# The chunked recurrence of a transformer block: its inverse's turned form made by transposes in each level

## The chip, the cores and the metric

One core of one Trainium2 chip runs the whole program in one launch. The metric is device time in microseconds, the median of three runs of the kernel. TensorE is called PE below, and its weight loads PEld; VectorE is DVE in the profile's rows, ScalarE ACT, GpSimd POOL.

## What is computed

The program is two transformer blocks over 512 tokens (with 256 context tokens in front in the second). One part of the second block's mixer is a linear recurrence with a removal term, run over 768 tokens in both directions for 8 heads of 64 dims:

```python
def wkv7_scan(state0, r, w, k, v, a_vec, b_vec, reverse):
    def step(S, inp):
        r_t, w_t, k_t, v_t, a_t, b_t = inp
        sa = jnp.einsum('bhij,bhj->bhi', S, a_t)
        S = (S * w_t[:, :, None, :] + sa[..., None] * b_t[:, :, None, :]
             + v_t[..., None] * k_t[:, :, None, :])
        return S, jnp.einsum('bhij,bhj->bhi', S, r_t)
```

The rest (norms, projections, three kinds of attention, experts) stands unchanged in both kernels.

## The kernel before, in words

Stage `Wkv` does this recurrence in 12 steps of 64 tokens. Within a step the 64 tokens depend on one another through a strictly triangular 64x64 matrix per head and direction, of which (1 - L) has to be inverted. There are 16 such matrices (4 pairs of heads `c`, 2 heads `e` of a pair, 2 directions `d`), kept in tiles of 128 partitions by 512 columns, and a group of 16 products of 64x64 works on all of them; in the trace a group is 32 matmul records. The inverse X is built in 5 levels: the blocks of L that join neighbours of size 2, 4, 8, 16, 32 (`lo`, made by GpSimd, "level_blocks") are multiplied by X (`half`, L2211), ScalarE copies the result out of PSUM (`t1`, L2373), a second product multiplies it by X from the other side (`grow`, L2224), and VectorE adds it to X (L2468). As a matmul takes its left operand transposed, `grow` needs X turned. So the kernel before keeps X twice: plain in `x` and turned in `xt`. `grow_turned` (L2232) makes the addition to `xt`, and VectorE adds it (L2471). The last level makes only the turned form.

Around the levels stand, in the order in which PE runs a step: three turns of value, replacement and key factors to token rows (`turn`, L2184, copied by ScalarE, L2369); `key_grams` (L2169, masked by VectorE, L2460); in level 0 `gram(2)` (L2161, mask L2420); in levels 1 to 4 products beside the half products that need only the state or the values (`w_from_state` L2250, `w_from_keys` L2274, `y_from_state` L2258); then the first two grams of the next step (L2161, masks L2420 and L2427), the solved values u (L2307), a turned gram of the next step (L2178, mask L2433), and the products into outputs and state (L2266, L2317, L2321, L2325). VectorE adds state (L2439) and outputs (L2452) and decays the state (L2445). VectorE also makes the factors of the next step: `removal` L2407, `reading` L2412, `replacement` L2416, `new_keys` L2402.

The order on each engine is the order of the code; semaphores with counts by step and place tie the engines (`at`, `wait`), and PE runs the steps as a loop, with waits against registers. In the kernel before, the tiles of `lo`, `x`, `xt` and `t1` have their two directions placed so (`home`) that the four products in a row use the four quarters of PE. PE's products onto the diagonal quarters alone (rows to the same columns, as in `grow_turned`) use two.

The level, on PE and on VectorE:

```python
for lv in range(self.LEVELS):
    half(lv)
    ...
    ready(lv)
    if lv < last_lv:
        grow(lv)
    grow_turned(lv)
```

## Time and profile before

| | us |
|---|---|
| median of 3 runs | 2858.52 (2855.38 to 2859.93) |
| the profiled execution | 2863.22 |
| its span, first to last instruction | 2861.4 |
| PE matmuls busy, share of the span | 2508.4, 88% |
| PE weight loads | 1945.2, 68% |
| VectorE | 1637.7, 57% |
| ScalarE | 1215.2, 42% |
| GpSimd | 426.4, 15% |
| mean granted clock of TensorE | 0.930 |

The profile is of one execution. Busy shares are averages over many stages; the stage `Wkv` stands at 1362 to 1644 us of the span, about a tenth of it, and only its own rows tell what bounds it. In a timeline row the first number is the start in us from the span's start, the second the time from the first instruction's start to the last one's end, then engine, line, operation, output and inputs, shape and count; in brackets the engine's idle time before and what ended it ("issue": nothing that the profile shows). PE's records overlap, so a group's time is longer than the distance to the next group's start.

### The profile page before, as it was taken

What the parts mean: (1) busy time and instruction counts of PE and PEld (TensorE: products, weight loads), DVE (VectorE), ACT (ScalarE), POOL (GpSimd) and SP (SyncE); (2) the same over time, 40 slices, a digit from 0 to 9 for tenths busy, and PEclk for the clock granted to TensorE, in tenths of its full rate; (3) what the DMA queues carried; (4) which work ended last, traced back from release to release, by engine and by line L of the source; (5) the groups of instructions that cost most, each with busy time, mean ns of one, the idle gap of its engine ahead of it and who ended that gap; (6) DMA issues with size and microseconds to landing.
All of it is one profiled execution on the core that took longest, in us unless ns stands there. A gap on an engine that the chain in (4) does not pass through costs nothing.

```text
span 2861.4 us, 55427 instructions
## 1 busy us (share of the span) xinstructions
PE 2508.4 (88%) x23264; PEld 1945.2 (68%) x23264; DVE 1637.7 (57%) x2360; ACT 1215.2 (42%) x1740; POOL 426.4 (15%) x412
## 2 busy tenths in 40 slices
PE   6979889999978779997888887899977889988996
PEld 5745577787857436785888765777766656767774
DVE  3655535555442274445566564588965355548895
ACT  2433333222231216424333324278864247446784
POOL 1010001000010020002455401122220030012221
PEclk9978989999999779998999988999988899999997
DMA  4246922222211000100000031199863100017995
GB/s 176 89 154 254 351 87 96 96 88 97 93 61 45 25 0 1 78 16 5 2 0 0 10 139 61 68 385 378 339 263 133 66 1 2 25 70 286 355 345 199
DMA packets 63892, 353.33 MB, mean 123 GB/s; under 512 B 15329, under 2 KB 15345, under 8 KB 27248
## 3 DMA queue, kind: packets, MB, share of 16 engines
q1 hardware_dynamic: 41792, 292.60, 26.9%
q0 software_dynamic: 21936, 58.50, 5.5%
q8 instruction: 109, 1.79, 0.2%
q14 instruction: 55, 0.45, 0.0%
HBM read 344.91 MB, written 36.70 MB: 133 GB/s over the span
## 4 chain that ended last, share of the span: by engine, by line
PE 72%; DVE 8%; ACT 5%; issue 4%; PEld 3%; DVEq 3%; DMA 2%; POOL 1%; POOLq 1%; ACTq 1%; PEldq 1%
PE psum L642 13%; PE psum L436 12%; PE psum L3271 9%; PE psum L3293 4%; PE psum L1187 4%; PE psum L1827 3%; PE psum L1206 3%; PE psum L1197 3%; PE psum L2882 2%; PEld psum L436 2%; PE psum L2232 2%; PE psum L1733 2%; PE psum L2211 1%; PE psum L3236 1%; PE psum L1045 1%
## 5 line engine op out<-in xcount | busy, mean ns | idle before, releaser
L436 PE MATMUL psum<-arena_r 128*128 128x512 f32 (+1 forms) x976 | 312.3, 361 | 4.3 <-DVE weight_slots_r L462 4.2
L642 PE MATMUL psum<-arena_r 128*128 128x512 f32 x704 | 250.8, 397 | 10.8 <-issue 4.0
L436 PE MATMUL psum<-arena_r,weight_slots_r 128*128 128x512 f32 (+1 forms) x696 | 249.1, 358 | 0.0
L457 ACT ACTIVATE arena_r<-weight_slots 128x1024 fp32r<-128x1024 f32 x73 | 76.4, 1057 | 334.5 <-PE psum L436 251.1
L642 PE MATMUL psum<-arena_r,weight_slots_r 128*128 128x512 f32 x528 | 209.1, 396 | 0.0
L436 PEld LDWEIGHTS psum<-arena_r 128*128 128x128 f32 x976 | 179.3, 190 | 36.0 <-issue 4.3
L436 PE MATMUL psum<-h_t_r,arena_r 128*128 128x512 f32 (+1 forms) x528 | 192.7, 365 | 0.0
L3225 DVE TENSOR_TENSOR weight_slots_r<-weight_slots,arena_r 128x2048 fp32r<-128x2048 f32 x78 | 177.6, 2290 | 20.1 <-ACT arena_r L3220 19.7
L3225 DVE TENSOR_TENSOR weight_slots_r<-weight_slots,h_t_r 128x2048 fp32r<-128x2048 f32 x72 | 163.9, 2290 | 20.9 <-ACT h_t_r L3220 20.8
L642 PEld LDWEIGHTS psum<-arena_r 128*128 128x128 f32 x704 | 133.8, 190 | 45.6 <-issue 13.6
L1271 DVE TENSOR_REDUCE stat<-psum 128x1 f32<-128x768 f32 (+1 forms) x112 | 98.7, 881 | 108.1 <-PE psum L1187 107.9
L3271 PE MATMUL psum<-weight_slots_r,arena_r 128*128 128x512 f32 x400 | 157.7, 394 | 0.0
L3220 ACT ACTIVATE arena_r<-weight_slots 128x2048 fp32r<-128x2048 f32 x78 | 148.2, 1919 | 17.4 <-DMA weight_slots<-in_weights 16.7
L436 PEld LDWEIGHTS psum<-arena_r,weight_slots_r 128*128 128x128 f32 x696 | 131.7, 189 | 20.3
L3220 ACT ACTIVATE h_t_r<-weight_slots 128x2048 fp32r<-128x2048 f32 x72 | 136.8, 1920 | 17.4 <-DMA weight_slots<-in_weights 16.9
L3271 PE MATMUL psum<-arena_r 128*128 128x512 f32 x416 | 132.2, 399 | 10.1 <-issue 7.5
L642 PE MATMUL psum<-h_t_r,arena_r 128*128 128x512 f32 x352 | 140.3, 399 | 0.0
L1187 PE MATMUL psum<-arena 64*128 64x384 f32 (+2 forms) x416 | 121.0, 532 | 8.6 <-POOL arena L1237 4.9
L3271 PE MATMUL psum<-h_t_r,arena_r 128*128 128x512 f32 x384 | 122.5, 400 | 5.7 <-issue 5.7
L642 PEld LDWEIGHTS psum<-arena_r,weight_slots_r 128*128 128x128 f32 x528 | 100.2, 190 | 22.6
L462 DVE TENSOR_TENSOR weight_slots_r<-weight_slots,arena_r 128x1024 fp32r<-128x1024 f32 x73 | 88.4, 1219 | 45.2 <-ACT arena_r L457 44.3
L3379 POOL DMA_INDIRECT arena<-h_rows,arena x50 | 71.7, 1435 | 274.1 <-PE psum L3236 190.0
(469 smaller groups left out, 5485.0 us busy)
## 6 DMA issues: line engine op xcount, KB each, us to landing
weight_slots<-in_weights SPq DMA_DIRECT2D x277, 1024.0 KB, 6.8
arena<-y_rows POOLq DMA_DIRECT2D x20, 512.0 KB, 7.9
h_rows<-arena POOLq DMA_DIRECT2D x10, 512.0 KB, 2.9
x_keep<-x_t POOLq DMA_DIRECT2D x1, 3072.0 KB, 9.0
x_t<-x_keep POOLq DMA_DIRECT2D x2, 1536.0 KB, 8.6
x_t<-in_x POOLq DMA_DIRECT2D x1, 2048.0 KB, 9.8
out_x<-x_t SPq DMA_DIRECT2D x1, 2048.0 KB, 7.2
arena<-in_toe POOLq DMA_DIRECT2D x1, 1792.0 KB, 7.3
```

The costliest lines, as they stand in the source:

```text
L436: last = self.nc.tensor.matmul(self.bank(n), w[:, kt, :], self.operand(part, kt, a, b), start=(i == 0), stop=(i == len(passes) - 1))
L462: self.nc.vector.tensor_tensor(out=self.tile_weights(self.kern.slots_r, t), in0=self.tile_weights(self.kern.slots, t), in1=self.w_hi[:, t ...
L642: last = nc.tensor.matmul(bank, w(p, k), x(q, k), start=(k == j == 0), stop=(k == n - 1 and j == 2))
L1187: last = t_.matmul(s[:, r, a:b], q, key[:, a:b], start=True, stop=True)
L1197: last = t_.transpose(self.turned_bank(u)[:, i * P:(i + 1) * P], self.probs[:, u % 2, i * P:(i + 1) * P], kern.ident)
L1206: last = t_.matmul(self.out_bank()[64 * e:64 * e + 64, :], self.units[u][2](i), self.probs_t[:, u % 4, i * P:(i + 1) * P], start=(i == 0), ...
L1271: v.reduce_max(kern.row_max[:, par], self.score_bank(u), mybir.AxisListType.XY)
L1827: last = self.nc.tensor.matmul(self.bank(n), w, x, start=(i == 0), stop=(i == len(pairs) - 1))
L3220: self.nc.scalar.activation(self.weights(item)[0], x, ACT.Copy).then_inc(self.rounded[0], 1)
L3225: self.nc.vector.tensor_tensor(out=self.kern.slots_r[:, slot, :], in0=self.kern.slots[:, slot, :], in1=hi.bitcast(F32), op=ALU.subtract).t ...
L3271: last = nc.tensor.matmul(ps[t % 2], x[:, t % 2, kt * P:(kt + 1) * P], w[:, k, :], start=(kt == 0 and i == 0), stop=(kt == KT - 1 and i == 2))
L3293: last = nc.tensor.matmul(ps[5 + half], x[:, t % 2, k * P:(k + 1) * P], w[:, k, half * 512:(half + 1) * 512], start=(k == 0 and i == 0), s ...
```

## The change

Only `Wkv` changes. X is kept plain alone. At the start of every level four 128x128 transposes on PE (`turned`) write X turned into PSUM bank 6, and VectorE copies that bank to `xt` when the half product is done (`turned_copied`); `grow` waits for this copy and for ScalarE's. `grow_turned`, its addition in each level, the turned gram of the next step and the second preset by GpSimd are gone; the last level multiplies onto the turned form and VectorE adds it to `xt`. The three turns, the key grams and the last gram move from the front of the step into the levels (`beside`): key grams at level 0, last gram and the turns of replacement factors and values at level 1, the keys' turn at level 3. The state product moves to level 2 and needs the decayed state; the value product stands whole at level 3. On VectorE the copies are new, removal stands in level 3, the new keys in level 2, the reading factor behind the first masks of the next step. GpSimd's `keyed` moves from level 2 to level 3. The placement by `home` is gone.

```diff
         def step(n, more):
             def half(lv):
-                if lv:
-                    wait("level_added", n, self.sum_of(lv - 1, 0))
-                else:
-                    wait("token_rows", n, 1)
-                wait("level_blocks", n, lv)
-                for c, e, d in units:
-                    last = t.matmul(bank_of(6, d, c, e, self.home(c, d)), self.plain(w.lo[lv % 2], c, e, d), self.plain(w.x, c, e, d),
-                                    start=True, stop=True)
+                for c in range(4):
+                    for e, d in corners:
+                        last = t.matmul(into(4, 0, d, c, e), self.by_token(w.lo[lv % 2], c, d, e), self.by_token(w.x, c, d, e),
+                                        start=True, stop=True)
                 last.then_inc(self.sem("level_half"), 1)
 
-            def ready(lv):
+            def turned():
+                for c in range(4):
+                    t.transpose(self.turned_bank()[:, c * P:(c + 1) * P], w.x[:, c * P:(c + 1) * P], ident)
+
+            def grow(lv):
                 wait("level_half_copied", n, lv)
-                if lv:
-                    wait("level_added", n, self.sum_of(lv - 1, 1))
-                else:
-                    wait("state", n, -2)
-
-            def grow(lv):
-                for c, e, d in units:
-                    last = t.matmul(bank_of(4, self.home(c, d), c, e, d), self.turned(w.xt, c, e, d), self.turned(w.t1, c, e, d),
-                                    start=True, stop=True)
+                wait("level_turned_copied", n, lv)
+                for c in range(4):
+                    for e, d in corners:
+                        if lv < last_lv:
+                            last = t.matmul(into(4, 0, e, c, d), self.by_dim(w.xt, c, d, e), self.by_dim(w.t1, c, d, e), start=True,
+                                            stop=True)
+                        else:
+                            last = t.matmul(self.by_dim(self.turned_bank(), c, d, e), self.by_dim(w.t1, c, d, e),
+                                            self.by_dim(w.xt, c, d, e), start=True, stop=True)
                 last.then_inc(self.sem("level_summed"), 1)
 
-            def grow_turned(lv):
...
-            wait("more_factors", n)
-            turn(6, w.vc)
-            turn(7, w.bt)
-            wait("y_added", n, -1)
-            turn(0, w.kt)
-            wait("masked", n, 2)
-            wait("read", n)
-            key_grams().then_inc(self.sem("more_grams"), 1)
-            for lv in range(self.LEVELS):
-                half(lv)
...
+            def beside(lv):
                 if lv == 0:
-                    wait("token_rows", n, 2)
-                    gram(2).then_inc(self.sem("last_grams"), 1)
+                    wait("more_factors", n)
+                    wait("read", n)
+                    wait("state", n, -2)
+                    key_grams().then_inc(self.sem("more_grams"), 1)
                 if lv == 1:
+                    wait("y_added", n, -1)
+                    last_gram().then_inc(self.sem("more_grams"), 1)
+                    wait("more_masked", n, 0)
+                    turn(3, w.bt)
+                    turn(2, w.vc)
+                if lv == 2:
                     w_from_state()
-                if lv == 2:
-                    w_from_keys(0)
                 if lv == 3:
-                    w_from_keys(1)
+                    w_from_keys()
+                    turn(2, w.kt)
                 if lv == last_lv:
                     y_from_state()
-                ready(lv)
-                if lv < last_lv:
-                    grow(lv)
-                grow_turned(lv)
+
+            for lv in range(self.LEVELS):
+                wait("level_blocks", n, lv)
+                if lv:
+                    wait("level_added", n, lv - 1)
+                turned()
+                half(lv)
+                beside(lv)
+                grow(lv)
             if more:
+                wait("token_rows", n, 2)
                 first_grams(n, 1)
...
+        def rows(n, i, bank, x):
+            act.wait_ge(*self.at("tokens", n, i))
+            s.activation(x, psum[:, bank, :], ACT.Copy).then_inc(self.sem("token_rows"), 1)
+
         def step(n):
-            for i, (bank, x) in enumerate(((6, w.vr), (7, w.br), (0, w.kr))):
-                act.wait_ge(*self.at("tokens", n, i))
-                s.activation(x, psum[:, bank, :], ACT.Copy).then_inc(self.sem("token_rows"), 1)
             more = n + 1 < self.STEPS
             for lv in range(self.LEVELS):
-                act.wait_ge(*self.at("level_half", n, lv))
-                s.activation(self.two(w.t1), self.by_rows(6), ACT.Copy).then_inc(self.sem("level_half_copied"), 1)
+                half_copied(n, lv)
                 if lv == 0 and more:
                     decays(n + 1)
-                if lv == 1 and more:
-                    growths(n + 1)
+                if lv == 1:
+                    if more:
+                        growths(n + 1)
+                    rows(n, 0, 3, w.br)
+                    rows(n, 1, 2, w.vr)
                 if lv == 2 and more:
                     scaled(n + 1, 0, 1, 2, 3)
                 if lv == 3:
-                    act.wait_ge(*self.at("w_summed", n, 2))
-                    s.activation(self.four(w.wv), self.by_head(0, 0), ACT.Copy).then_inc(self.sem("w_copied"), 1)
-            act.wait_ge(*self.at("u_summed", n))
-            s.activation(self.two(w.uv), self.by_rows(6), ACT.Copy).then_inc(self.sem("u_copied"), 1)
+                    act.wait_ge(*self.at("solve_summed", n, 1))
+                    s.activation(self.four(w.wv), self.pair(0, 0), ACT.Copy).then_inc(self.sem("solve_copied"), 1)
+                    rows(n, 2, 2, w.kr)
...
+        def turned_copied(n, lv):
+            dve.wait_ge(*self.at("level_half", n, lv))
+            v.tensor_copy(w.xt, self.turned_bank()).then_inc(self.sem("level_turned_copied"), 1)
+
+        def grown(n, lv):
+            dve.wait_ge(*self.at("level_summed", n, lv))
+            if lv < self.LEVELS - 1:
+                last = v.tensor_tensor(out=self.four(w.x), in0=self.four(w.x), in1=self.pair(4, 0), op=ALU.add)
+            else:
+                last = v.tensor_tensor(out=w.xt, in0=w.xt, in1=self.turned_bank(), op=ALU.add)
+            last.then_inc(self.sem("level_added"), 1)
...
         def step(n):
             more = n + 1 < self.STEPS
-            dve.wait_ge(*self.at("more_grams", n))
-            for i, (dst, m) in enumerate(((w.lkt, w.strict), (w.rkt, w.incl))):
-                v.tensor_tensor(out=self.four(dst), in0=self.key_grams(i), in1=spread(m), op=ALU.mult)
-            dve.drain().then_inc(self.sem("more_masked"), 1)
             for lv in range(self.LEVELS):
+                turned_copied(n, lv)
                 if lv == 0:
-                    dve.wait_ge(*self.at("last_grams", n))
-                    mask(2, w.rbt, w.incl).then_inc(self.sem("more_masked"), 1)
-                if lv < self.LEVELS - 1:
-                    dve.wait_ge(*self.at("level_summed", n, self.sum_of(lv, 0)))
-                    v.tensor_tensor(out=self.two(w.x), in0=self.two(w.x), in1=self.by_rows(4), op=ALU.add).then_inc(
-                        self.sem("level_added"), 1)
-                dve.wait_ge(*self.at("level_summed", n, self.sum_of(lv, 1)))
-                v.tensor_tensor(out=w.xt, in0=w.xt, in1=psum[:, 3, :], op=ALU.add).then_inc(self.sem("level_added"), 1)
-                if lv in (1, 2) and more:
-                    if lv == 1:
-                        dve.wait_ge(*self.at("exps", n + 1))
-                        dve.wait_ge(*self.at("w_summed", n, 0))
-                    removal(n + 1, lv - 1)
+                    key_masks(n)
+                if lv == 3 and more:
+                    removal(n + 1)
+                grown(n, lv)
+                if lv == 1:
+                    last_mask(n)
+                if lv == 2 and more:
+                    new_keys(n + 1)
                 if lv == 3 and more:
                     replacement(n + 1)
             if more:
-                dve.wait_ge(*self.at("w_summed", n, 3))
-                reading(n + 1, 0)
-                reading(n + 1, 1)
-                dve.drain().then_inc(self.sem("read"), 1)
                 low(n + 1)
-                new_keys(n + 1)
-                up(n + 1)
+                reading(n + 1)
             state(n)
             outputs(n)
             decayed(n)
...
         def keyed(n):
             if n:
-                pool.wait_ge(*self.at("last_grams", n - 1))
+                pool.wait_ge(*self.at("tokens", n - 1, 1))
...
-                if lv == 2 and n + 1 < self.STEPS:
+                if lv == 3 and n + 1 < self.STEPS:
                     keyed(n + 1)
```

PE at the front of a step and in level 0, before (L2201 are waits against registers; L2184 are the turns, L2169 the key grams, L2211 the half product):

```order
L2201 REGISTER_ALU [waits wkv_more_factors]
L2184 MATMUL psum<-consts,arena 128x128 x8
L2201 REGISTER_ALU [waits wkv_y_added]
L2184 MATMUL psum<-consts,arena 128x128 x4
L2201 REGISTER_ALU [waits wkv_masked]
L2201 REGISTER_ALU [waits wkv_read]
L2169 MATMUL psum<-rstd,arena 64x128 x16
L2201 REGISTER_ALU [waits wkv_token_rows]
L2201 REGISTER_ALU [waits wkv_level_blocks]
L2211 MATMUL psum<-arena 64x64 x16
```

And now (L2164 the waits; L2181 are the transposes, L2175 the half product, L2139 the key grams, L2189 the growth):

```order
L2164 REGISTER_ALU [waits wkv_level_blocks]
L2181 MATMUL psum<-consts,arena 128x128 x4
L2175 MATMUL psum<-arena 64x64 x16
L2164 REGISTER_ALU [waits wkv_more_factors]
L2164 REGISTER_ALU [waits wkv_read]
L2164 REGISTER_ALU [waits wkv_state]
L2139 MATMUL psum<-rstd,arena 64x128 x16
L2164 REGISTER_ALU [waits wkv_level_half_copied]
L2164 REGISTER_ALU [waits wkv_level_turned_copied]
L2189 MATMUL psum<-arena 64x64 x16
```

The half product stood behind three turns and the key grams; it now stands behind four transposes alone, and the key grams stand between it and the growth.

PE in level 1 before, from the wait for the addition (L2250 the state product, L2224 the growth, L2232 the turned growth):

```order
L2201 REGISTER_ALU [waits wkv_level_added]
L2201 REGISTER_ALU [waits wkv_level_blocks]
L2211 MATMUL psum<-arena 64x64 x16
L2201 REGISTER_ALU [waits wkv_more_masked]
L2250 MATMUL psum<-arena,rstd 64x64 x16
L2201 REGISTER_ALU [waits wkv_level_half_copied]
L2201 REGISTER_ALU [waits wkv_level_added]
L2224 MATMUL psum<-arena 64x64 x16
L2232 MATMUL psum<-arena 64x64 x16
```

And now (L2146 the last gram, L2152 the turns of replacement factors and values):

```order
L2164 REGISTER_ALU [waits wkv_level_blocks]
L2164 REGISTER_ALU [waits wkv_level_added]
L2181 MATMUL psum<-consts,arena 128x128 x4
L2175 MATMUL psum<-arena 64x64 x16
L2164 REGISTER_ALU [waits wkv_y_added]
L2146 MATMUL psum<-rstd,arena 64x64 x16
L2164 REGISTER_ALU [waits wkv_more_masked]
L2152 MATMUL psum<-consts,arena 128x128 x8
L2164 REGISTER_ALU [waits wkv_level_half_copied]
L2164 REGISTER_ALU [waits wkv_level_turned_copied]
L2189 MATMUL psum<-arena 64x64 x16
```

Four transposes stand between the addition and the half product, the last gram and two turns between the half product and the growth, and the turned growth is gone.

VectorE from the masks of the next step's grams to the first addition, before (L2420 and L2427 masks, L2402 new keys, L2433 the turned gram's mask, L2439 state, L2452 outputs, L2445 decay, L2460 key masks, L2420 last gram's mask):

```order
L2420 TENSOR_TENSOR arena<-psum,x_t 128x512 [waits wkv_grams]
L2427 COPY_PREDICATED arena<-x_t,psum 128x512 [waits wkv_presets]
L2402 TENSOR_TENSOR arena<-arena 128x4x64 [waits keys_weighed]
L2402 TENSOR_TENSOR arena<-arena 128x4x64
L2433 COPY_PREDICATED arena<-x_t,psum 128x512 [waits wkv_presets,wkv_grams]
L2439 TENSOR_TENSOR arena<-arena,psum 128x512 [waits wkv_state_summed]
L2452 TENSOR_TENSOR h_t<-h_t,psum 128x4x64 [waits wkv_outputs]
L2452 TENSOR_TENSOR h_t<-h_t,psum 128x4x64
L2445 TENSOR_TENSOR arena<-arena 128x512
L2460 TENSOR_TENSOR arena<-psum,x_t 128x512 [waits wkv_more_grams]
L2460 TENSOR_TENSOR arena<-psum,x_t 128x512
L2420 TENSOR_TENSOR arena<-psum,x_t 128x512 [waits wkv_last_grams]
```

And now (L2397 and L2400 masks, L2386 reading, L2429 state, L2441 outputs, L2434 decay, L2416 the copy of the turned form, L2406 key masks, L2421 the addition):

```order
L2397 TENSOR_TENSOR arena<-psum,x_t 128x512 [waits wkv_grams]
L2400 COPY_PREDICATED arena<-x_t,psum 128x512 [waits wkv_presets]
L2386 TENSOR_TENSOR rstd<-arena 128x4x64 [waits wkv_solve_summed]
L2386 TENSOR_TENSOR rstd<-arena 128x4x64
L2429 TENSOR_TENSOR arena<-arena,psum 128x512 [waits wkv_state_summed]
L2441 TENSOR_TENSOR h_t<-h_t,psum 128x4x64 [waits wkv_outputs]
L2441 TENSOR_TENSOR h_t<-h_t,psum 128x4x64
L2434 TENSOR_TENSOR arena<-arena 128x512
L2416 COPY arena<-psum 128x512 [waits wkv_level_half]
L2406 TENSOR_TENSOR arena<-psum,x_t 128x512 [waits wkv_more_grams]
L2406 TENSOR_TENSOR arena<-psum,x_t 128x512
L2421 TENSOR_TENSOR arena<-arena,psum 128x512 [waits wkv_level_summed]
```

The copy of the turned form and the key masks stand between the decay and the first addition, and the reading factor now stands behind the two masks.

## Rows read from the trace of the kernel before

**Rows 1.** Windows, two stretches: us, busy time and count by engine, PE clock, DMA share, GB/s

```profile
1385.00:1410.00 25.00, 21.88 (x912) 20.36 (x904) 15.49 (x28) 8.32 (x16) 12.11 (x14) 0.95 0.00 1
...
1456.00:1479.00 23.00, 20.04 (x875) 18.61 (x867) 14.77 (x27) 8.22 (x16) 12.99 (x15) 1.00 0.00 0
```

**Rows 2.** Timeline of VectorE: the state additions of steps 1, 2, 3 and 12

```profile
1385.16 0.69 DVE L2439 TENSOR_TENSOR arena<-arena,psum 128x512 f32<-128x512 f32 x1 [2.02 <-PE psum L2321]
...
1409.39 0.68 DVE L2439 TENSOR_TENSOR arena<-arena,psum 128x512 f32<-128x512 f32 x1
...
1432.65 0.67 DVE L2439 TENSOR_TENSOR arena<-arena,psum 128x512 f32<-128x512 f32 x1
...
1640.23 0.69 DVE L2439 TENSOR_TENSOR arena<-arena,psum 128x512 f32<-128x512 f32 x1 [2.23 <-PE psum L2321]
```

**Rows 3.** Timeline, all engines: level 1 of one step, links of the chain

```profile
1462.30 0.69 PE L2211 MATMUL psum<-arena 64*64 64x64 f32 x32
...
1463.06 0.60 ACT L2373 ACTIVATE arena<-psum 128x512 f32<-128x512 f32 x1 [2.13 <-PE psum L2211]
...
1463.88 0.69 PE L2224 MATMUL psum<-arena 64*64 64x64 f32 x32 [0.41 <-ACT arena L2373]
...
1464.63 0.69 DVE L2468 TENSOR_TENSOR arena<-arena,psum 128x512 f32<-128x512 f32 x1 [1.64 <-PE psum L2224]
...
1465.55 0.69 PE L2211 MATMUL psum<-arena 64*64 64x64 f32 x32
```

**Rows 4.** Timeline, all engines: the last level and the tail of that step

```profile
1472.04 0.69 PE L2211 MATMUL psum<-arena 64*64 64x64 f32 x32
...
1473.61 1.09 PE L2232 MATMUL psum<-arena 64*64 64x64 f32 x30
...
1474.81 0.69 DVE L2471 TENSOR_TENSOR arena<-arena,psum 128x512 f32<-128x512 f32 x1 [1.49 <-PE psum L2232]
...
1475.42 0.75 DVE L2412 TENSOR_TENSOR rstd<-arena 128x256 f32<-128x256 f32 x2
...
1475.63 0.69 PE L2307 MATMUL psum<-x_t,arena 64*64 64x64 f32 x32
...
1476.97 0.71 DVE L2427 COPY_PREDICATED arena<-x_t,psum 128x512 f32<-128x512 int32 x1
...
1477.81 0.69 PE L2317 MATMUL psum<-arena 64*64 64x64 f32 x32 [0.55 <-DVE arena L2427]
...
1478.77 0.68 PE L2325 MATMUL psum<-arena,x_t 64*64 64x64 f32 x32
```

**Rows 5.** Timeline, all engines: the front of that step

```profile
1455.51 0.68 PE L2325 MATMUL psum<-arena,x_t 64*64 64x64 f32 x32
...
1456.66 1.34 PEld L2184 LDWEIGHTS psum<-consts,arena 128*128 128x128 f32 x12 [0.62 <-issue]
...
1457.58 0.93 DVE L2445 TENSOR_TENSOR arena<-arena 128x512 f32<-128x512 f32 x1 [0.17 <-issue]
1458.17 0.86 PEld L2169 LDWEIGHTS psum<-rstd,arena 64*64 64x64 f32 x32 [0.17 <-issue]
...
1459.10 0.64 PE L2211 MATMUL psum<-arena 64*64 64x64 f32 x32
1459.35 1.29 DVE L2460 TENSOR_TENSOR arena<-psum,x_t 128x512 f32<-128x512 f32 x2 [0.84 <-PE psum L2169]
...
1460.75 0.69 DVE L2420 TENSOR_TENSOR arena<-psum,x_t 128x512 f32<-128x512 f32 x1
```

**Rows 6.** One line's instructions, another stage: VectorE's plain copies out of PSUM

```profile
L502 DVE COPY arena<-psum x25: 681/692/693, 65.1 to 2265.2; 128x512 f32<-128x512 f32 x17, 64x512 f32<-64x512 f32 x8
```

**Rows 7.** Timelines of PE and of its weight loads: end of the first step

```profile
1383.03 0.63 PE L2266 MATMUL psum<-arena 64*64 64x64 f32 x27 [1.89 <-issue]
...
1384.83 1.15 PE L2325 MATMUL psum<-arena,x_t 64*64 64x64 f32 x30
...
1385.91 1.99 PEld L2184 LDWEIGHTS psum<-consts,arena 128*128 128x128 f32 x12
```

More of the change, by code:

```diff
@@ L2303, in step @@
             if more:
+                wait("token_rows", n, 2)
                 first_grams(n, 1)
-            wait("level_added", n, self.sum_of(last_lv, 1))
-            for c, e, d in units:
-                last = t.matmul(bank_of(6, self.home(c, d), c, e, d), self.turned(w.xt, c, e, d), self.turned(w.wv, c, e, d),
-                                start=True, stop=True)
-            last.then_inc(self.sem("u_summed"), 1)
-            if more:
-                turned_gram().then_inc(self.sem("grams"), 1)
@@ L2322, in step @@
+            for c in range(4):
+                for e, d in corners:
+                    t.matmul(s_of(c, d, e), self.by_token(w.kr, c, d, e), self.by_token(w.vr, c, d, e), start=(c == 0), stop=False)
+            wait("solve_copied", n, 1)
+            for c in range(4):
+                for e, d in corners:
+                    last = t.matmul(s_of(c, d, e), self.by_token(w.br, c, d, e), self.by_token(w.uv, c, d, e), start=False, stop=(c == 3))
             last.then_inc(self.sem("state_summed"), 1)
@@ L2417, in replacement @@
             dve.drain().then_inc(self.sem("factors"), 1)
-        def mask(i, dst, m):
-            return v.tensor_tensor(out=self.four(dst), in0=self.by_head(*self.GRAMS[i]), in1=spread(m), op=ALU.mult)
         def low(n):
@@ L2489, in step @@
             decayed(n)
-        dve.wait_ge(*self.at("exps", 0))
-        for d in (0, 1):
-            removal(0, d)
-            reading(0, d)
-        dve.drain().then_inc(self.sem("read"), 1)
+        removal(0)
+        reading(0)
         replacement(0)
@@ L2543, in key_totals @@
             pool.drain().then_inc(self.sem("key_totals"), 1)
[L2545 to L2546 removed]
+        preset(0)
         keyed(0)
```

215 lines of the change are left out of this document (95 added, 120 removed).

## Prediction, before the changed kernel was timed

> **What bounds the kernel now.** I read the windows first: a step of the recurrence lasts 23.3 us, TensorE (PE) is busy for 20 of each 23 at the full granted clock, and no transfer runs [rows 1]. The state additions then give the period: from 1409.39 to 1432.65 is 23.26 us, and eleven periods run from 1385.16 to 1640.23 [rows 2]. Last I followed one step in the timeline. Busy engines do not bound it; one chain does, handed around between PE, ScalarE and VectorE. All engines are in this one stage, so what a step gains or loses the kernel gains or loses.
>
> In a middle level the links are [rows 3]: half product to ScalarE's copy 0.76 (1462.30 to 1463.06), copy to growth product 0.82, growth to VectorE's addition 0.75, addition to the next half product 0.92; together 3.25. The turned growth and its addition lie beside this chain: the addition that follows L2468 at 1464.63 starts at the next half product and is needed only by the growth after that. So what the change removes in levels 0 to 3 was covered, and its removal is worth nothing to the chain. Only at the last level does the turned growth stand on it [rows 4].
>
> **The change part by part.** I count one steady step, and call the start of its last output products (1455.51, L2325 [rows 5]) zero.
>
> *Transposes in the chain.* Each level now begins with four 128x128 transposes, and they wait for the addition as the half product did, so they go in front of it. Twelve such weight loads take 1.34 us, 0.112 each, and the first 64-row load behind them waits another 0.17 [rows 5]. Four cost 4 x 0.112 + 0.17 = 0.62 as an upper end; a third of the 1.51 from 1456.66 to 1458.17 gives 0.50 as a lower one. I take 0.60, since the 0.17 belongs to a change of shape and not to a count.
>
> *VectorE's copy.* The growth now waits for ScalarE's copy (0.60 us) and for VectorE's copy of the turned form, both started by the half product. A VectorE copy of 512 f32 out of PSUM takes 0.69 [rows 6], so VectorE ends last by 0.09; with handing on I take copy to growth as 0.92, the addition's link, instead of 0.82: 0.10 more. Removal, new keys and replacement stand between these copies in VectorE's order, each a tile's worth like the reading factor's 0.75 [rows 4]; VectorE has 0.92 + 0.75 us between a copy and its addition and more behind it, so they stay hidden.
>
> *A middle level* is then 0.60 + 0.76 + 0.92 + 0.75 + 0.91 = 3.94, 0.69 over 3.25.
>
> *Level 1 holds more.* Between half product and growth PE runs last_gram and two turns: 0.47 + 0.47 + 8 x 0.112 + 0.17 = 2.01 (a group of 32 records issues in about 0.47: two stand between 1477.81 and 1478.77 [rows 4]). The growth could have started at 0.76 + 0.92 = 1.68, so it is held 0.33. A change of shape from 64-row products to transposes stands nowhere in the trace with PE busy before it; I bound it by 0 and the 0.17 of the other direction, and take 0.10: held 0.43, level 1 costs 1.12 in all. The Trainium skill, "TensorEngine Tiling (Array Packing)", Key Properties, says that every change of the tiling mode drains TensorE; the trace agrees with it in the one direction that it shows, 0.17. By it the other direction costs the same, and the step's sum is 0.1 to 0.2 higher, some 2 us on the kernel. Level 3 (value product and one turn: 0.47 + 0.47 + 0.45 + 0.17 + 0.10 = 1.66) stays under 1.68: 0.69. The state product of level 2 (now each row half onto itself, as the turned growth is, whose group takes 1.09 of records against 0.69 [rows 4], so about 0.9 to issue) ends at 1.4: hidden.
>
> *The front of the step.* Three turns and the key products (1456.66 to 1459.10, where the half product starts) leave it, some 2.4 us of PE. What is late next is VectorE: state, outputs, decay, and only behind these the copy of the turned form. The decay starts at 2.07 and takes 0.93 [rows 5], so the copy starts at 3.1 and the growth at 3.1 + 0.92 = 4.0. The key masks follow the copy 0.6 later (two of VectorE's operations in a row start 0.61 apart, 1474.81 and 1475.42 [rows 4]) and take 1.40 until the next operation starts (1459.35 to 1460.75 [rows 5]), so the addition starts at 5.1, and the half product of level 1 at 5.1 + 0.91 + 0.60 = 6.61. Before it started at 1462.30, which is 6.79. The front gains 0.18, not 2.4.
>
> *Last level and tail.* Half product 4 to u product is 3.59 now (1472.04 to 1475.63 [rows 4]); after, 0.76 + 0.92 + 1.20 + 0.82 = 3.70: 0.11 more. From u to the last output products takes 3.14 (1475.63 to 1478.77), because VectorE does the reading factor (1475.42) before its two masks and the state's products wait for the second mask (1476.97 to 1477.81 is 0.84). The reading now comes behind the masks: the growth of level 4 starts 2.02 before u, issues for 0.9, the two gram groups follow, and the second lands 0.76 after its start, so the masks start 0.1 after u, the second at 0.75; state products at 1.59, last outputs at 2.53. Gain 0.61. The turned gram and its mask go as well; they were covered.
>
> *Sum for a step:* -0.18 + 1.12 + 0.69 + 0.69 + 0.11 - 0.61 = +1.82 us; twelve steps make **+21.8 us**. ScalarE, GpSimd and transfers cost nothing: ScalarE's row copies fall where it waits; GpSimd's key factors move one level later and wait for a turn, yet are used two levels on; no step issues a transfer, and SP's queue is untouched.
>
> *The clock.* PE was dense in every steady step. Now it stands still from about 2.5 to 4.0, runs one growth, and stands still again to 6.0: some 0.7 us of records in 3.5. In the first step PE stopped for 1.89 us; right behind it the last output products took 1.15 instead of 0.68 and the twelve weight loads 1.99 instead of 1.34, and the windows beside it show 0.95 [rows 1, 5, 7]: part of these stretches was granted the lower level, 1.2 GHz. That cost the second step 24.23 (1385.16 to 1409.39) against 23.26: 0.97 us. So the price is between 0 and 0.97 a step. As PE now idles longer than in the one row that shows a fall, but not in every step at the same moment, I take nine steps of twelve: 9 x 0.97 = **+8.7 us**.
>
> Against the profiled execution, 2863.22 us, the sum is 2863.2 + 21.8 + 8.7 = 2893.7. That execution lies 4.7 over the median of the three runs; on the median, 2858.52, it is **2889**.
>
> **The rivals.**
>
> *The clock holds.* PE was granted 1.00 in all steps from 1410 on with pauses of up to 0.6 us, and nothing shows that 1.5 us already matter. Then +21.8 alone: 2880. With the lower bounds (0.50 for the transposes in four levels, no cost for the unseen change of shape, 0.6 a step less) it is 2874.
>
> *The clock falls inside the levels too.* The twelve transposes of a step run amid products at 1.00 and are too few to show anything. If transposes do not keep the clock up, a level has only two groups in 3.94 us. At the lower level a level is dearer by about two groups and four transposes, 0.47 + 0.47 + 0.45 = 1.4; over five levels and twelve steps 84, so at half of them +42: 2858.5 + 21.8 + 42 = 2922. The Trainium skill, "TensorE: Matmul & The Clock Gate", Part 4, says that a transpose does not count as busy in the way a product does; by it this rival is the likely course. Against it stands that every level keeps its products and no pause in levels 2 to 4 exceeds 1 us.
>
> *The front is worth what it held.* Place: the copy of the turned form at level 0. If VectorE reached it at 1.84, when the half product lands (0.48 + 0.60 + 0.76), instead of 3.1, and the key masks came behind the addition, the growth would start at 2.76 and the next half product, by 0.75 + 0.91 + 0.50, at 4.92: 1.87 gained instead of 0.18. With the lower ends for the rest (transposes 0.50, nothing for the unseen change of shape, VectorE's copy no later than ScalarE's) the step is -1.87 + 0.83 + 0.49 + 0.49 + 0.01 - 0.61 = -0.66, twelve steps -8: 2851. It decides where the copy of level 0 starts: at about 2.5 the change is even, by the same lower ends. Against it: the order on VectorE puts decay before the copy in every step, and the durations of [rows 5] leave no room.
>
> **How the numbers follow.** Likeliest: sum with the clock falling in most steps, 2889, chance 0.58. Clock holds, 2880: 0.25. Clock falls in the levels, 2922: 0.10. Front worth its size, 2851 or no change: 0.07. A range of 2874 to 2905 takes in the first two with their bounds (upper: 0.97 in all twelve steps, 0.17 for the unseen change, and a little of the third) and leaves out the rest. About 0.2%, 5.7 us, is what a measurement of this kernel tells from no change. Faster by more than that 0.04, within it 0.03, slower 0.93.
>
> **What would show it.** State additions 25.0 to 26 us apart; half products 3.9 apart from level 2 to 3 and 4.4 from level 1 to 2; growth at level 0 started by VectorE's copy behind the decay; additions of level 0 ready behind the key masks; some stretches behind level 0 with groups of 64x64 products at double duration. It is wrong if the front shortens by over 1 us, if a level takes under 3.6, if transposes overlap with the addition before them, or if ScalarE or GpSimd ends a wait on this chain.

## The result and the profile after

The changed kernel takes 2913.18 us, median of 4 runs (2910.63 to 2918.62), beside 2859.22 of the kernel before, median of 4: a ratio of 1.0193, 95% interval 1.0173 to 1.0212. It is slower, as forecast, but by 54.0 us where 30.5 were predicted, and it lies above the range of 2874 to 2905. The profiled execution took 2918.62 us, its span 2916.5.

The time went into the recurrence: up to the first state addition the two profiled executions differ by 0.4 us (1385.16 before, 1385.58 now), behind the last one by 0.1. Line numbers below are those of the changed kernel: L2181 transposes, L2175 half product, L2189 growth, L2416 copy of the turned form, L2421 addition, L2386 reading factor, L2434 decay, L2519 GpSimd's lo products. First the chain that ended last, for the front of one step (start, us, what):

```profile
1497.82 1.42 DVE rstd L2386
...
1499.36 0.69 DVE arena L2429
...
1501.06 1.71 DVE arena L2434
...
1502.88 0.70 DVE arena L2416
...
1503.70 1.16 PE psum L2189 x32
...
1505.71 1.09 PE psum L2181 x4
1506.80 1.06 PE psum L2175 x32
1507.86 0.85 PE psum L2146 x32
1508.71 1.78 PE psum L2152 x8
```

Two things are new in it. A reading factor stands on the chain ahead of the state's addition, and it and the decay take far longer than in [rows 4, 5]. Behind the growth, four transposes take 1.09 and the two turns (eight 128x128 products) 1.78. Over all steps the two VectorE products look like this (line view: min/median/max ns, first and last start, forms):

```profile
L2386 DVE TENSOR_TENSOR rstd<-arena x24: 410/1102/1498, 1353.5 to 1666.7; 128x256 f32<-128x256 f32 x24
L2434 DVE TENSOR_TENSOR arena<-arena x12: 692/1712/1800, 1387.3 to 1698.0; 128x512 f32<-128x512 f32 x12
```

The same instruction takes 0.41 us in one place and 1.10 to 1.50 in others (a half of the reading), or 0.69 and 1.71 (the decay). What runs beside it is in the timelines of VectorE and GpSimd for the same step:

```profile
1496.11 0.72 DVE L2400 COPY_PREDICATED arena<-x_t,psum 128x512 f32<-128x512 int32 x1
1496.73 2.51 DVE L2386 TENSOR_TENSOR rstd<-arena 128x256 f32<-128x256 f32 x2
1499.36 0.69 DVE L2429 TENSOR_TENSOR arena<-arena,psum 128x512 f32<-128x512 f32 x1
1499.96 0.92 DVE L2441 TENSOR_TENSOR h_t<-h_t,psum 128x256 f32<-128x256 f32 x2
1501.06 1.71 DVE L2434 TENSOR_TENSOR arena<-arena 128x512 f32<-128x512 f32 x1 [0.17 <-issue]
...
1496.27 2.69 POOL L2519 TENSOR_TENSOR arena<-arena,x_t 128x512 f32<-128x512 f32 x2 [1.95 <-DVE arena L2397]
1498.92 1.79 POOL L2505 TENSOR_TENSOR h_t<-h_t,arena 128x256 f32<-128x256 f32 x2
1500.95 1.26 POOL L2519 TENSOR_TENSOR arena<-arena,x_t 128x512 f32<-128x512 f32 x1 [0.25 <-issue]
```

The lo products end at 1498.96 and 1502.21; the reading ends at 1499.24, the decay at 1502.77, 0.28 and 0.56 behind. The mask, the state's addition and the outputs, which read one operand out of PSUM, keep their times (0.72, 0.69, 0.92) with GpSimd work beside them. TensorE from level 2 of this step to level 1 of the next:

```profile
1484.16 0.69 PE L2175 MATMUL psum<-arena 64*64 64x64 f32 x32
...
1487.88 0.69 PE L2175 MATMUL psum<-arena 64*64 64x64 f32 x32
...
1491.69 0.69 PE L2175 MATMUL psum<-arena 64*64 64x64 f32 x32
...
1495.28 0.69 PE L2265 MATMUL psum<-x_t,arena 64*64 64x64 f32 x32
...
1497.92 0.68 PE L2285 MATMUL psum<-arena,x_t 64*64 64x64 f32 x32
...
1503.70 1.13 PE L2189 MATMUL psum<-arena 64*64 64x64 f32 x32 [2.42 <-DVE arena L2416]
1505.71 1.09 PE L2181 MATMUL psum<-consts,arena 128*128 128x128 f32 x4 [0.87 <-DVE arena L2421]
1506.73 1.13 PE L2175 MATMUL psum<-arena 64*64 64x64 f32 x32
```

Levels 2 to 4 are a little shorter than predicted: half products 3.72 and 3.81 apart (predicted 3.94), the last to the solved values u 3.59 (3.70). From u to the last output products it takes 2.64, a little longer than the predicted 2.53. Behind the idle 2.42 every group takes 1.6 to 1.7 times as long. The windows say at which clock (columns as in [rows 1]): levels 2 to 4 with the tail, then the growth of level 0 to the growth of level 1, then the whole stage:

```profile
1484.16:1497.92 13.76, 11.48 (x494) 10.39 (x497) 8.51 (x15) 4.94 (x10) 4.75 (x5) 1.00 0.00 0
...
1503.70:1510.43 6.73, 5.85 (x109) 5.03 (x109) 2.45 (x4) 1.72 (x3) 1.28 (x1) 0.51 0.01 1
...
1386.00:1695.00 309.00, 231.14 (x7992) 200.87 (x7996) 186.49 (x277) 90.11 (x170) 125.68 (x135) 0.90 0.00 0
```

1.00 is the level of 2.4 GHz and 0.51 that of 1.2 GHz; in [rows 1] a steady step was granted 1.00. State additions run from 1385.58 to 1695.39, eleven periods of 28.16 on average. The prediction with its clock term makes 25.8 of a steady step of 23.25; the mean of the eleven before was 23.19 [rows 2].

### The profile page after: what moved, and what is told of

Its sections match the earlier page's. It is cut to its first block, busy times and chain, and to the rows that moved or that the text cites. A ratio compares the mean times of both kernels' runs of the same rounds, so it can differ in the third digit from the quotient of the medians.

```text
span 2916.5 us, 52044 instructions
## 1 busy us (share of the span) xinstructions
PE 2515.5 (86%) x21584; PEld 1935.5 (66%) x21584; DVE 1664.4 (57%) x2360; ACT 1217.5 (42%) x1740; POOL 415.6 (14%) x400
## 4 chain that ended last, share of the span: by engine, by line
PE 71%; DVE 11%; ACT 4%; issue 3%; PEld 3%; DVEq 3%; DMA 2%; POOL 1%; ACTq 1%; PEldq 0%; POOLq 0%; SPq 0%
PE psum L642 13%; PE psum L436 12%; PE psum L3233 9%; PE psum L3255 4%; PE psum L1187 4%; PE psum L1827 3%; PE psum L1206 3%; PE psum L1197 3%; PE psum L2844 2%; PEld psum L436 2%; PE psum L1733 2%; PE psum L3198 1%; PE psum L1045 1%; PE psum L2181 1%; PE psum L2175 1%
```

## The experiments

Three theories stood. **C**: VectorE's products that read only SBUF lose time beside GpSimd. **K**: time is lost to TensorE's low clock behind the front of the step. **S**, the prediction's own: the transposes stand on the chain. Below, a step is the distance between two state additions; the last period is shorter in every kernel, so means are of all eleven and steady steps are compared with steady ones. The kernel before had a median of 2859.55 us beside the first four kernels, 2859.48 beside the next four and 2857.31 beside the last.

**Two waits for GpSimd.**

```diff
                 if lv == 0:
                     pool.wait_ge(*self.at("masked", n, 0))
+                    if n:
+                        pool.wait_ge(*self.at("read", n))
+                elif lv == 1:
+                    if n:
+                        pool.wait_ge(*self.at("state", n - 1, 1))
```

> Two waits are added on GpSimd: its first lo product of a step waits until VectorE has made the step's reading factor, its second (and with it the key totals) until VectorE has multiplied the state by its decay. Theory C: in the changed kernel VectorE's products that read only SBUF are slowed by GpSimd's work beside them (the two halves of the reading factor 1.10 and 1.49 us instead of 0.41 each in the first step, the decay 1.71 instead of 0.69). Then both fall back, about 0.42 a half and 0.69, the addition into the state starts 1.1 us earlier after the last output products begin, the copy of the turned form 2.1 us earlier, and 12 steps give some 25 us: 2888 us if the low clock at level 1 stays what it was, about 2875 if it goes with the shorter wait. Theory K, that the low TensorE clock after the idle front makes all of the unexpected time and GpSimd only happens to run there: the two durations stay near 2.5 and 1.7 and the time near 2913, or a little more for the later lo products.

Measured: 2870.61 us (10 runs), ratio to before 1.0038 (1.0024 to 1.0051). The line view, and TensorE behind the output products, which started at 1504.90:

```profile
L2386 DVE TENSOR_TENSOR rstd<-arena x24: 404/413/429, 1349.2 to 1626.3; 128x256 f32<-128x256 f32 x24
L2434 DVE TENSOR_TENSOR arena<-arena x12: 691/693/694, 1384.3 to 1653.4; 128x512 f32<-128x512 f32 x12
...
1508.49 0.69 PE L2189 MATMUL psum<-arena 64*64 64x64 f32 x32 [0.30 <-DVE arena L2416]
1510.49 0.63 PE L2181 MATMUL psum<-consts,arena 128*128 128x128 f32 x4 [1.31 <-DVE arena L2421]
1511.05 0.69 PE L2175 MATMUL psum<-arena 64*64 64x64 f32 x32
```

Nothing but waiting was added, and 43 us came back. Every reading and decay has its own duration again, the growth of level 0 starts 3.59 behind the output products instead of 5.78, and transposes and half product are back at 0.63 and 0.69. A steady step takes 24.15; the mean of the eleven, from 1382.64 to 1650.99, is 24.40. Two of them take 25.7, and the windows give the first of these a lower clock:

```profile
1431.20:1456.87 25.67, 20.44 (x749) 17.87 (x744) 14.74 (x26) 8.37 (x16) 11.78 (x14) 0.93 0.00 0
```

C holds, and most of the clock's cost went with it.

**Filler for TensorE.** 48 products a step that nothing reads, L2199, where TensorE idles in level 0:

```diff
                     key_grams().then_inc(self.sem("more_grams"), 1)
+                    filler(32)
...
                 grow(lv)
+                if lv == 0:
+                    filler(16)
```

> 48 products of 64x64 that nothing reads are added in every step on TensorE where it idles in level 0: 32 behind the key products, 16 behind the growth. Theory K (TensorE runs at 1.2 GHz in the transposes, half product, last gram and turns of level 1 because it idled ahead of them): these groups return to 0.35, 0.48 and 0.47 us in most steps, and 1.2 to 1.5 us a step come back, some 15 us: 2898 us. Theory C alone (the waits of VectorE make all of it): the reading and the decay keep 2.5 and 1.7 us, and the time stays at 2913, or rises by up to 6 where a filler stands ahead of a product that is due. In both theories reading and decay are not changed.

Measured: 2889.83 us, ratio 1.0106 (1.0078 to 1.0134). The windows over the stage, and TensorE at level 1:

```profile
1383.00:1650.00 267.00, 221.91 (x8424) 198.12 (x8416) 178.10 (x265) 84.34 (x161) 123.03 (x132) 1.00 0.00 0
...
1494.22 0.63 PE L2181 MATMUL psum<-consts,arena 128*128 128x128 f32 x4 [0.39 <-DVE arena L2430]
1494.78 0.69 PE L2175 MATMUL psum<-arena 64*64 64x64 f32 x32
...
1496.89 0.69 PE L2189 MATMUL psum<-arena 64*64 64x64 f32 x32
```

The granted clock is 1.00 and the groups are short again, while the reading (median 1.10 a half) and the decay (1.72) stay long, and the growth of level 0 still starts 5.78 behind the output products (1492.22 behind 1486.44). A steady step takes 26.35 (1382.46 to 1408.81), the mean of the eleven is 26.18 (1382.46 to 1670.45). So K is real too, 28.16 - 26.18 = 1.98 us a step in the mean. Steady steps of this run and of the two waits differ by 26.35 - 24.15 = 2.20, which is C without the clock; the start of the growth differs by as much (5.78 - 3.59).

**Both.** The two waits, and 16 + 16 filler products.

> Both GpSimd waits, and 16 products that nothing reads behind the key products and 16 behind the growth of level 0. Is there clock time left once VectorE is not slowed? Theory: the low clock at level 1 was a consequence of the longer idle time, so filler adds nothing beyond the two slow steps (25.7 instead of 24.15): 2867 to 2871 us, each step 24.15 or 0.2 more where a filler stands in the way. If the two costs were independent, the 1.8 us a step that filler gave alone would come off here too: 2850.

Measured: 2866.35 us, ratio 1.0022 (1.0006 to 1.0038); steady steps of 24.15, from 1549.94 to 1574.09, and a mean of 24.11 over the eleven (1380.60 to 1645.83). With the waits in place the filler gives only 24.40 - 24.11 = 0.29 a step, where it gave 1.98 without them. So most of the clock's cost is not a second, independent one: it follows from the idle time that C makes.

**One wait.** Only the first of the two, the one for the reading.

> Only the first of the two GpSimd waits: the first lo product waits for the reading factor, the second lo product and the key totals run beside the decay again. It splits what the two waits gave together (28.16 us a step to 24.15 in the steps without a slow stretch). Theory C: the reading returns to 0.41 a half, the decay stays near 1.6, the copy of the turned form comes 0.9 to 1.0 us later than with both waits: steps of 25.1 us if TensorE stays at 2.4 GHz, 2882 us. If the longer idle ahead of the first growth is what lets the clock fall (theory K as the consequence of C), the steps stand at 26.5 to 27 and the time near 2900.

Measured: 2871.05 us, ratio 1.0042 (1.0028 to 1.0055): level with both waits, and 11 us under the forecast of 2882. The decay did not stay at 1.6 as expected; VectorE's decay and GpSimd beside it:

```profile
1511.16 0.83 DVE L2434 TENSOR_TENSOR arena<-arena 128x512 f32<-128x512 f32 x1 [0.17 <-issue]
...
1508.93 2.52 POOL L2521 TENSOR_TENSOR arena<-arena,x_t 128x512 f32<-128x512 f32 x2 [3.31 <-DVEq L2387]
1511.39 2.07 POOL L2505 TENSOR_TENSOR h_t<-h_t,arena 128x256 f32<-128x256 f32 x2
```

The second lo product ends at 1511.45 and the decay 0.54 behind it, although GpSimd's key totals (L2505) start at once: now these take longer (2.07 instead of 1.59 with both waits). A slower rate beside any GpSimd work does not explain a decay of 0.83 here and 1.71 above. What agrees is the distance between the two ends, 0.54 here and 0.56 above.

**GpSimd's product in pieces.** Each lo product of levels 0 to 2 as four of a quarter of the columns:

```diff
-                g_.tensor_tensor(out=w.lo[lv % 2].rearrange("p (a t) -> p a t", a=8), in0=w.lt.rearrange("p (a t) -> p a t", a=8),
-                                 in1=m, op=ALU.mult).then_inc(self.sem("level_blocks"), 1)
+                pieces = 4 if lv < 3 else 1
+                for i in range(pieces):
+                    a = slice(8 // pieces * i, 8 // pieces * (i + 1))
+                    last = g_.tensor_tensor(out=w.lo[lv % 2].rearrange("p (a t) -> p a t", a=8)[:, a, :],
+                                            in0=w.lt.rearrange("p (a t) -> p a t", a=8)[:, a, :], in1=m[:, a, :], op=ALU.mult)
+                last.then_inc(self.sem("level_blocks"), 1)
```

> The changed kernel with GpSimd's lo products of the first three levels each issued as four products of a quarter of the columns; no wait is added, and as much is computed. It tells apart how VectorE loses time beside GpSimd. Blocked (a product of VectorE that reads two SBUF operands waits until the GpSimd product that runs when it comes has ended, then takes its own 0.41 or, for the decay, about 0.55 more; in the traces so far the decay ends 0.55 us behind the end of the lo product beside it, in the kernel before too): it then waits for a quarter, some 0.3 us at most, so the reading's halves take 0.5 to 0.8 us instead of 1.10 and 1.49, the decay 0.7 to 1.0 instead of 1.71, GpSimd's pieces stretch instead, and 1.3 to 1.9 us a step come back besides what the clock gives: 2880 to 2892 us. Shared rate (both run, VectorE at two fifths of its rate while GpSimd works): halves and decay stay at 1.1 to 1.5 and 1.6 to 1.7, 2913 us or more.

Measured: 2869.57 us, ratio 1.0040 (1.0024 to 1.0056), 10 us under the blocking theory's 2880 to 2892, which left out what the clock gives; the stage was granted 0.99.

```profile
L2386 DVE TENSOR_TENSOR rstd<-arena x24: 412/676/699, 1349.8 to 1627.9; 128x256 f32<-128x256 f32 x24
L2434 DVE TENSOR_TENSOR arena<-arena x12: 691/692/1048, 1385.0 to 1654.8; 128x512 f32<-128x512 f32 x12
```

GpSimd computes the same in smaller instructions, and the halves of the reading fall from 1.10 and 1.49 to about 0.68, without a semaphore between the two engines. A half still ends 0.28 behind the end of a GpSimd instruction, but that is now a piece: it starts at 1504.20 and takes 0.70, beside a piece that starts at 1504.15 and takes 0.46. A shared rate would have left the halves long. VectorE waits until the GpSimd product under way has ended.

**The reading moved late in the kernel before.** The two halves of the reading stand behind the masks there, as in the changed kernel:

```diff
+                low(n + 1)
                 dve.wait_ge(*self.at("w_summed", n, 3))
                 reading(n + 1, 0)
                 reading(n + 1, 1)
                 dve.drain().then_inc(self.sem("read"), 1)
-                low(n + 1)
```

> The kernel before, with the two reading products moved behind the two masks (low), where GpSimd's lo products run, as the changed kernel has them. Theory C: the two halves take about 2.5 us together instead of 0.75, the addition into the state starts some 2.5 us later, and 12 steps cost about 25 us: 2884 us. Without a slowdown beside GpSimd the move alone costs 0.3 us a step, what the reading keeps of the state's wait: 2863 us.

Measured: 2859.05 us, ratio 1.0008 (0.9994 to 1.0022), where C was to give 2884. A miss, and no test of C: the move does not bring the reading beside a lo product.

```profile
1470.33 0.74 DVE L2412 TENSOR_TENSOR rstd<-arena 128x256 f32<-128x256 f32 x2
...
1472.12 1.27 POOL L2535 TENSOR_TENSOR arena<-arena 128x512 f32<-128x512 f32 x1 [1.85 <-issue]
1473.56 2.95 POOL L2556 TENSOR_TENSOR arena<-arena,x_t 128x512 f32<-128x512 f32 x2 [0.18 <-issue]
```

In that kernel GpSimd's key factors (L2535) stand ahead of the lo products (L2556) in its order and wait for the new keys, so the lo products start 3.2 us after the reading, not with the masks. The changed kernel makes the new keys earlier, in level 2 instead of the tail; that, and not the reading's place alone, is what puts the two side by side. In the one step of this run in which the decay comes early in a lo product, the first (decay at 1379.93), it takes 1.66 instead of 0.94.

**Transposes twice.** `turned()` issued twice in every level.

> The changed kernel with the four transposes of each level issued twice. Prices the transposes on the chain. Theory S (what the prediction used: the transposes stand on the path from one addition to the next half product in levels 1 to 4, beside the front in level 0): 4 times 0.44 us a step more, +21 us, 2934 us. If they hide beside another wait, 2913. If more transposes let the clock fall further, above 2940; if the longer busy stretch lets it rise, below 2925.

Measured: 2937.02 us, ratio 1.028 (1.0245 to 1.0314), 23.8 us over the changed kernel where 21 were forecast. The window over the stage, and TensorE at the start of level 2:

```profile
1387.00:1625.00 238.00, 186.36 (x5990) 165.18 (x5992) 135.46 (x203) 66.95 (x127) 95.41 (x103) 0.89 0.00 0
...
1514.42 1.06 PE L2181 MATMUL psum<-consts,arena 128*128 128x128 f32 x8 [0.89 <-DVE arena L2422]
1515.41 0.69 PE L2175 MATMUL psum<-arena 64*64 64x64 f32 x32
```

S holds with its price: eight take 1.06 where four took 0.63, 0.43 more on the chain of each level at the full clock; in level 1, at the low one, they take 1.94 (at 1507.16) instead of 1.09. Twenty more transposes a step did not lift the granted clock (0.89 against 0.90).

**A front without the waits.** The two waits above are left out. The reading stands between the copy and the addition of the last level, the decay between copy and addition of level 0, the key masks behind that addition. GpSimd's key factors now wait for the reading and its key totals for the decay (not in the excerpt).

```diff
                 turned_copied(n, lv)
-                if lv == 0:
-                    key_masks(n)
+                if lv == 0 and n:
+                    decayed(n - 1)
...
+                if lv == 4 and more:
+                    reading(n + 1)
                 grown(n, lv)
+                if lv == 0:
+                    key_masks(n)
```

> Built on the theory that VectorE's chain ahead of the first growth bounds the front of the changed kernel (reading, addition, outputs, decay, copy of the turned form): the reading stands in the last level between the copy and the last addition, the decay between copy and addition of level 0, the key masks behind that addition; GpSimd's keys (more_factors) wait for the reading and its key totals for the decay, so that neither runs beside a product that reads only SBUF. The growth of level 0 should start about 0.9 us earlier behind the last output products than with the GpSimd waits alone (3.6 us there): steps of 23.0 to 23.2 us, 2858 us, level with the kernel before. If the front is bound by something else (key products, half copy, TensorE) the steps stay at 24.1 and the time near 2870.

Measured: 2852.83 us, ratio 0.9978 (0.9963 to 0.9992), 0.2% under the kernel before. Steady steps take 22.97 (1541.49 to 1564.46). With the output products at 1495.29:

```profile
1498.13 0.69 PE L2189 MATMUL psum<-arena 64*64 64x64 f32 x32
1499.70 0.63 PE L2181 MATMUL psum<-consts,arena 128*128 128x128 f32 x4 [0.88 <-DVE arena L2421]
```

The growth starts 2.84 behind them, and TensorE no longer idles for VectorE ahead of it.

**Front and tail.** The front version, with the first grams in other banks, so that the state's products need not wait for the masks:

```diff
-    GRAMS = ((2, 0), (2, 256))
+    GRAMS = ((4, 0), (4, 256))
...
                 if lv:
                     wait("level_added", n, lv - 1)
+                else:
+                    wait("masked", n, 1)
...
-            if more:
-                wait("masked", n, 3)
-            else:
+            if not more:
                 wait("token_rows", n, 2)
```

> As the front version, and the first grams stand in banks 4 and 5 as in the kernel before, so that the key products of the state at the step's end don't wait for the two masks any longer (0.7 us of TensorE's idle time ahead of them in the changed kernel). Then the state's products wait for the copy of u instead: 0.4 to 0.6 us a step less than the front version, 22.5 to 22.7, some 2853 us, faster than both kernels. If the copy of u is as late as the masks: no difference to the front version.

Measured: 2843.00 us (7 runs), ratio 0.9938 (0.9918 to 0.9957): 0.6% under the kernel before, and so under both kernels. The mean step is 22.40 (eleven from 1378.81 to 1625.19), against 23.19 before, which makes 8.7 us of the 16.5. Where the rest lies no run shows; outside the stage the profiled executions differ by several us among themselves (the first state addition stands at 1378.81 here and at 1380.66 in the front version, at 1385.16 before).

## Why the prediction was wrong, point by point

The sign was right and its reason, S, was right: doubling the transposes showed that they stand on the chain. Two terms of the sum failed, and both made it too small.

**The front of the step: a duration taken without its neighbour.** The prediction wrote that "The decay starts at 2.07 and takes 0.93 [rows 5], so the copy starts at 3.1", and in the tail it moved the reading behind the masks without asking for its length there. Both read only SBUF, and neither price was looked at against GpSimd. Measured: reading 2.51, decay 1.71, copy at 4.96 and growth at 5.78 instead of 4.0; 2.20 us a steady step by the filler run against the two waits. The tail's gain, priced at 0.61, did come (0.50, u to the last output products 2.64 for 3.14), and it was paid back at the next addition. The sentence "ScalarE, GpSimd and transfers cost nothing" looked for what waits on GpSimd by semaphore, and no semaphore shows this wait. One of the prediction's own signs of being wrong, that GpSimd ends a wait on this chain, is what happened.

The kernel before had it in view. Its line view, and GpSimd's two lo products beside the decay of [rows 5]:

```profile
L2445 DVE TENSOR_TENSOR arena<-arena x12: 692/939/950, 1387.1 to 1643.3; 128x512 f32<-128x512 f32 x12
...
1456.69 1.27 POOL L2556 TENSOR_TENSOR arena<-arena,x_t 128x512 f32<-128x512 f32 x1 [0.18 <-issue]
...
1457.92 1.72 POOL L2556 TENSOR_TENSOR arena<-arena,x_t 128x512 f32<-128x512 f32 x1
```

The first lo product ends at 1457.96 and the decay at 1457.58 + 0.93 = 1458.51, 0.55 behind; in the last step, with nothing beside it, the decay took 0.69. So 0.93 held the rest of a wait. The next lo product there took 1.72 instead of 1.27: it waited for the decay in turn. The reading's row had a sign as well: one half in the kernel before took 0.62 instead of 0.42 (at 1350.15), beside a GpSimd copy.

**The clock: the term was there and too small.** It was 0.97 in nine steps of twelve, 0.73 a step; measured is 1.98 in the mean step. The price came from a pause of 1.89 and was to hold for a predicted pause of 1.5. With C the pause was 2.42, and the low level lasted from the growth through transposes, half product, last gram and turns. With the two waits, where that pause was 0.30, the clock still cost 24.40 - 24.11 = 0.29 a step. So most of this term hung on the failed one.

**Structure: overpriced.** A steady step is 24.15 - 23.25 = 0.90 longer with the two waits, where +1.82 stood. Of the difference 0.46 is the front (half product of level 1 at 6.15 behind the outputs, 6.61 predicted), about half of it the decay at 0.69 for 0.93. Levels came out 0.1 to 0.2 cheaper: an addition to the half product takes 1.38 (1486.50 to 1487.88), not 0.91 + 0.60 = 1.51. The change of shape that no row showed cost what was taken for it: half product to growth in level 1 is 2.11 with the filler (1494.78 to 1496.89), as 2.01 + 0.10 said.

Together, in means over the eleven periods (23.19 before, 24.11 with waits and filler, 26.18 with filler alone, 28.16 changed): 0.92 for the structure, 2.07 for C and 1.98 for the clock, 4.97 a period and 54.7 in eleven. They add up by themselves, as differences along one row of kernels; which cost goes under which name depends on that row, since most of the clock's follows from C. Predicted were 1.82 + 0.73 a step. That the overpriced structure covered a part of what was missed is luck; it brought the forecast nearer to the measured time.

**The rivals.** "The clock holds" fell: the stage was granted 0.90. "The clock falls inside the levels too" named 2922, near the time, but not the course: groups of levels 2 to 4 kept 0.69 at a granted 1.00. The Trainium skill, "TensorE: Matmul & The Clock Gate", Part 4, on which it leaned, says that transposes do not count as busy in the way products do; the doubled transposes at 0.89 agree as far as they go. "The front is worth what it held" was not this kernel's course, but its condition, the copy at 1.84 instead of 3.1, is nearly what the front version made (2.02, 1497.31 behind 1495.29), and that one came out at 2852.83, near the 2851 named. What the prediction lacked was a rival in which an operation, at its new place, is held by what another engine runs beside it.

## What to carry to other kernels

Before a duration is carried to a new place, look at its minimum and maximum over the trace and at what GpSimd does beside the long ones. In this case a VectorE product with two SBUF operands that meets a GpSimd product under way waits for the rest of that product, and no semaphore names the wait. Moving an operation changes what other queues run beside it, so follow GpSimd's order too: what stands ahead of the product there, and what that waits for. A pause that grows on the chain can cost twice, once by itself and once by TensorE's clock behind it; price the pause first, then the clock. Three remedies worked here: a wait that keeps the two products apart, GpSimd's product split into pieces, and VectorE's product moved to another place, with GpSimd's work held off there.

## What the runs showed that was not expected

VectorE's wait is for the product under way, and is not a slower rate. The end comes a fixed time behind the end of GpSimd's product: 0.28 for a product that takes 0.41 alone (1497.82 behind 1496.27 + 1.27 = 1497.54, 1499.24 behind 1498.96) and 0.54 to 0.56 for one that takes 0.69 (changed kernel, kernel before, one wait). Quartering GpSimd's product shortened the wait without a semaphore. The Trainium skill, "SBUF — State Buffer", section "SBUF: two separate sides", states this: the pair of SBUF ports that VectorE and GpSimd share is an exclusive lock for a whole instruction, taken by whoever starts first, and on VectorE's side an instruction with two SBUF inputs needs it. The runs agree, in both directions (GpSimd's 1.72 for 1.27). By that rule the reading's price at its new place would have been the rest of the lo product beside it.
